# Products of 256 tokens with both parts of x side by side: ffn1's up product and three of four groups of the deep down products

## What is computed

```
def swiglu_ffn(h, w_in, w_out):                 # first block
    a, g = jnp.split(h @ w_in, 2, axis=-1)
    return (jax.nn.silu(a) * g) @ w_out

def gated_conv_ffn(x, w_gate, w_up, conv_w, conv_b, w_down):   # second block
    g = causal_dwconv3(x @ w_gate, conv_w) + conv_b
    return (jax.nn.silu(g) * (x @ w_up)) @ w_down
```

## Time and profile before

| | |
|---|---|
| time, median of 3 runs | 1600.87 us (1599.76 to 1603.91) |
| the profiled execution's own time | 1600.98 us |
| its span (first to last instruction) | 1599.8 us |
| mean granted TensorE clock | 0.994 of full speed |
| busy: PE, DVE, ACT | 98%, 56%, 43% |
| matmuls | 11195, about as many weight loads |
| chain that ended last | PE 88%, DVE 4%, ACT 2%, POOL 2% |

### The profile page before, as it was taken

One profiled execution on the slowest core, in us unless ns is written; L12 is line 12 of the kernel. 1 busy time (PEld: TensorE's weight loads), 2 busy tenths in 40 slices (PEclk: granted clock), 3 DMA queues, 4 the chain that ended last, 5 costly groups with the idle time before them and its releaser, 6 DMA issues.

```text
span 1599.8 us, 25708 instructions
## 1 busy us (share of the span) xinstructions
PE 1560.6 (98%) x11195; PEld 1386.1 (87%) x11195; DVE 901.0 (56%) x1176; ACT 682.0 (43%) x923; POOL 88.0 (6%) x124
## 2 busy tenths in 40 slices
PE   6999999999999999999999999999999999999998
PEld 4778866867888888878768999999999999999998
DVE  5422477463333433357866655568777656677763
ACT  4312476342212322235764444544545446555552
POOL 2210052000000000000000000034000000000000
PEclk8999999999999999999999999999999999999999
DMA  9864532745533232364134555565555554555551
GB/s 334 249 192 158 142 31 20 263 136 187 179 105 105 80 105 74 98 230 152 54 112 153 177 192 172 176 213 173 171 186 182 189 180 155 166 180 185 178 173 71
DMA packets 242976, 251.19 MB, mean 157 GB/s; under 512 B 4797, under 2 KB 240672, under 8 KB 242864
## 3 DMA queue, kind: packets, MB, share of 16 engines
q1 hardware_dynamic: 240080, 244.33, 46.2%
q0 software_dynamic: 2464, 5.09, 2.6%
q10 hardware_dynamic: 320, 0.13, 0.0%
HBM read 248.49 MB, written 1.05 MB: 156 GB/s over the span
## 4 chain that ended last, share of the span: by engine, by line
PE 88%; DVE 4%; ACT 2%; POOL 2%; issue 1%; DMA 1%; SPq 1%; DVEq 0%; ACTq 0%; POOLq 0%
PE psum L354 86%; PE psum L846 2%; DMA pre<-in_ada_w 1%; DVE sums L909 1%; POOL ptmp L1736 1%; DVE pt L923 1%; ACT wh L333 1%; DVE wl L340 1%; SPq L289 0%; DMA raw<-in_ada_w 0%; POOL ptmp L1735 0%; ACT scr L876 0%; DVE acc L1515 0%; POOL scr L1743 0%; ACT xh L624 0%
## 5 line engine op out<-in xcount | busy, mean ns | idle before, releaser
L354 PE MATMUL psum<-xh,wh 128*128 128x256 f32 (+1 forms) x1936 | 615.8, 318 | 5.0 <-DVE xl L668 2.8
L354 PE MATMUL psum<-xl,wh 128*128 128x256 f32 (+1 forms) x1936 | 609.3, 315 | 0.0
L354 PE MATMUL psum<-xh,wl 128*128 128x256 f32 (+1 forms) x1936 | 609.1, 315 | 0.0
L340 DVE TENSOR_TENSOR wl<-raw,wh 128x2048 fp32r<-128x2048 f32 (+1 forms) x186 | 419.1, 2254 | 273.1 <-ACT wh L333 272.9
L333 ACT ACTIVATE wh<-raw 128x2048 fp32r<-128x2048 f32 (+1 forms) x186 | 348.2, 1874 | 389.8 <-PE psum L354 385.0
L354 PEld LDWEIGHTS psum<-xh,wh 128*128 128x128 f32 x1936 | 370.2, 191 | 37.8 <-issue 10.0
L354 PEld LDWEIGHTS psum<-xh,wl 128*128 128x128 f32 x1936 | 370.2, 191 | 22.6
L354 PEld LDWEIGHTS psum<-xl,wh 128*128 128x128 f32 x1936 | 370.4, 191 | 21.9 <-issue 0.7
L354 PE MATMUL psum<-ah,wh 128*128 128x256 f32 (+1 forms) x704 | 217.9, 310 | 0.0
L354 PE MATMUL psum<-ah,wl 128*128 128x256 f32 (+1 forms) x704 | 217.9, 310 | 0.0
L354 PE MATMUL psum<-al,wh 128*128 128x256 f32 (+1 forms) x704 | 217.9, 310 | 0.0
(11 more groups left out here) (254 smaller groups left out, 1568.2 us busy)
## 6 DMA issues: line engine op xcount, KB each, us to landing
raw<-in_ffn_w_in SPq DMA_DIRECT2D x44, 1024.0 KB, 4.9
raw<-in_ada_w SPq DMA_DIRECT2D x25, 1024.0 KB, 5.3
pre<-in_ada_w SPq DMA_DIRECT2D x23, 1024.0 KB, 9.9
raw<-in_w_ffn_gate SPq DMA_DIRECT2D x22, 1024.0 KB, 5.2
raw<-in_w_ffn_up SPq DMA_DIRECT2D x22, 1024.0 KB, 5.2
raw<-in_ffn_w_out SPq DMA_DIRECT2D x16, 1024.0 KB, 5.0
raw<-in_w_ffn_down SPq DMA_DIRECT2D x16, 1024.0 KB, 5.0
raw<-in_na_w_qkv SPq DMA_DIRECT2D x12, 1024.0 KB, 5.6
```

The source lines that it names most:

```text
L340: dve.e.tensor_tensor(wl[:, c % NSPL, 0:z], raw[:, p % NRAW, 0:z], wh[:, c % NSPL, 0:z].bitcast(F32), ALU.subtract).then_inc(W.lo, 1)
L354: return pe.e.matmul(o, l, r, start=start, stop=stop, skip_group_check=shared)
```

## The change

Low and high part of x are placed side by side in one tensor (`x5`, `a1`; the addresses are those that they had). A new `group_wide` moves both at once: a matmul of the weights' high block by 512 columns (high part of x, then low part) into a whole bank, and one of the weights' low block by 256 columns into the first half of the same bank. So two matmuls and two weight loads stand where three and three stood; the number of columns is the same. The two halves of a bank have to be added afterwards, and the two halves m of a group now take a bank each.

It is used for the 22 groups of ffn1's up product and for the first three groups of D1, D2 and D3. The fourth group stays as it was, in bank 6 or as `DBANKS` says. ffn1's groups turn through three pairs of banks in place of six banks, and PE waits for the sum of group g-3. ACT and DVE now have work in every slot: in an even one ACT copies the second half bank into `scr`, DVE adds the first half to it, ACT takes tanh of the sum, DVE (tanh + 1) * a; in an odd one ACT copies the second half of g, DVE adds, DVE multiplies, ACT makes the high part, DVE the low part. In the down products DVE adds each half of the bank to the residual in turn. Some waits of later stages on banks are moved to match.

```diff
+        def group_wide(o, cs, x, ready, k_outer=False):
+            total, k0 = sum(weights[c][1] for c in cs), 0
+            for c in cs:
+                h, l = taken(c)
+                nk = weights[c][1]
+                for k, m in [(k, m) for k in range(nk) for m in range(2)] if k_outer else [(k, m) for m in range(2) for k in range(nk)]:
+                    ready(k0 + k)
+                    w = slice(m * P, (m + 1) * P)
+                    mm(o[m].rearrange("p (s n) -> p s n", s=2), h[:, k, w], x[:, :, k0 + k, :], k0 + k == 0, False, True)
+                    last = mm(o[m][:, 0:T], l[:, k, w], x[:, 0, k0 + k, :], False, k0 + k == total - 1, True)
+                last.then_inc(W.used, 1)
+                k0 += nk
...
 def down_pe(d, ready, ks=None):
             for i in range(4):
                 d.free(i)
-                group_T(halves(d.banks[i]), d.chunks(i), d.src[0], d.src[1], T, ready, k_outer=i == 0, ks=ks)
+                if d.wide is not None and i < 3:
+                    group_wide([psum[:, d.banks[i] + m, :] for m in range(2)], d.chunks(i), d.wide, ready, k_outer=i == 0)
+                    continue
+                group_T(halves(bank[d.banks[i]]), d.chunks(i), d.src[0], d.src[1], T, ready, k_outer=i == 0, ks=ks)
...
 def down_dve(d):
-                b = d.banks[i]
-                if d.gates is None:
+                b = bank[d.banks[i]]
+                if d.wide is not None and i < 3:
+                    parts = [psum[:, d.banks[i]:d.banks[i] + 2, s * T:s * T + T] for s in range(2)]
+                    for s in range(2):
+                        if s:
+                            dve.wait_ge(DN.half, d.at.half + d.per * (i + 1))
+                        done = DN.res if s else DN.half
+                        if d.gates is None:
+                            dve.e.tensor_tensor(pair(hT, i), parts[s], pair(hT, i), ALU.add).then_inc(done, 1)
+                        else:
+                            for m in range(2):
+                                k = 2 * i + m
+                                dve.e.scalar_tensor_tensor(hT[:, k, 0:T], parts[s][:, m, :], mod_col(*d.gates, k, 0), hT[:, k, 0:T], ALU.mult,
+                                                           ALU.add).then_inc(done, 1)
+                elif d.gates is None:
...
 def ffn1_pe():
             for g in range(22):
-                if g >= 6:
-                    pe.wait_ge(G1.g1 if g % 2 == 0 else G1.g2, (g - 6) // 2 + 1)
-                group_T(halves(ring[g]), [where["up1", g]], xh5, xl5, T, lambda k: pe.wait_ge(N.xl, 48 + k + 1), k_outer=g == 0)
+                if g >= 3:
+                    pe.wait_ge(G0.sum1 if (g - 3) % 2 == 0 else G0.sum2, (g - 3) // 2 + 1)
+                group_wide([bank[pairs1[g]], bank[pairs1[g] + 1]], [where["up1", g]], x5, lambda k: pe.wait_ge(N.xl, 48 + k + 1), k_outer=g == 0)
...
 def ffn1_act():
                 split_for(split_hi, c)
-                if g % 2:
-                    s = scr[:, p % 6, :]
-                    act.wait_ge(W.used, c + 1)
-                    if p >= 6:
-                        act.wait_ge(G1.lo, p - 5)
-                    act.e.activation(s, ring[g - 1][:, :], ACT.Tanh, scale=0.5).then_inc(G1.tanh, 1)
-                    act.wait_ge(G1.g2, p + 1)
-                    act.e.activation(ah1[:, 2 * p:2 * p + 2, :].rearrange("p k n -> p (k n)"), s, ACT.Copy).then_inc(G1.hi, 1)
+                act.wait_ge(W.used, c + 1)
+                if g % 2 == 0:
+                    t, u = tiles1(p)
+                    if p >= 3:
+                        act.wait_ge(G0.lo, 22 + p - 2)
+                    act.e.activation(two(t), parts1(g)[1], ACT.Copy).then_inc(G0.copy1, 1)
+                    act.wait_ge(G0.sum1, p + 1)
+                    act.e.activation(u, t, ACT.Tanh, scale=0.5).then_inc(G0.tanh, 1)
+                else:
+                    t, u = tiles1(p)
+                    act.wait_ge(G0.g1, 22 + p + 1)
+                    act.e.activation(two(u), parts1(g)[1], ACT.Copy).then_inc(G0.copy2, 1)
+                    act.wait_ge(G0.g2, 22 + p + 1)
+                    act.e.activation(ah1[:, 2 * p:2 * p + 2, :].rearrange("p k n -> p (k n)"), t, ACT.Copy).then_inc(G0.hi, 1)
             down_act(D1)
...
 def ffn1_dve():
-                if g % 2:
-                    s = scr[:, p % 6, :]
-                    dve.wait_ge(G1.tanh, p + 1)
-                    dve.e.scalar_tensor_tensor(s, s, 1.0, ring[g - 1][:, :], ALU.add, ALU.mult).then_inc(G1.g1, 1)
-                    dve.wait_ge(G1.g1, p + 1)
-                    dve.e.scalar_tensor_tensor(s, s, 0.5, ring[g][:, :], ALU.mult, ALU.mult).then_inc(G1.g2, 1)
-                    dve.wait_ge(G1.hi, p + 1)
-                    hi, lo = (t[:, 2 * p:2 * p + 2, :].rearrange("p k n -> p (k n)") for t in (ah1, al1))
-                    dve.e.tensor_tensor(lo, s, hi.bitcast(F32), ALU.subtract).then_inc(G1.lo, 1)
+                t, u = tiles1(p)
+                if g % 2 == 0:
+                    dve.wait_ge(G0.copy1, p + 1)
+                    dve.e.tensor_tensor(two(t), parts1(g)[0], two(t), ALU.add).then_inc(G0.sum1, 1)
+                    dve.wait_ge(G0.tanh, 22 + p + 1)
+                    dve.wait_ge(G0.sum1, p + 1)
+                    dve.e.scalar_tensor_tensor(t, u, 1.0, t, ALU.add, ALU.mult).then_inc(G0.g1, 1)
+                else:
+                    dve.wait_ge(G0.copy2, p + 1)
+                    dve.e.tensor_tensor(two(u), parts1(g)[0], two(u), ALU.add).then_inc(G0.sum2, 1)
+                    dve.wait_ge(G0.sum2, p + 1)
+                    dve.e.scalar_tensor_tensor(t, t, 0.5, u, ALU.mult, ALU.mult).then_inc(G0.g2, 1)
+                    dve.wait_ge(G0.hi, 22 + p + 1)
+                    hi, lo = (x[:, 2 * p:2 * p + 2, :].rearrange("p k n -> p (k n)") for x in (ah1, al1))
+                    dve.e.tensor_tensor(lo, t, hi.bitcast(F32), ALU.subtract).then_inc(G0.lo, 1)
```

More of the change, by code:

```diff
@@ L166, in program @@
         mixh1, mixl1 = at(0, "mixh1", [P, KT, T], F32R), at(8, "mixl1", [P, KT, T], F32R)
-        ah3, al3 = at(0, "ah3", [P, FT, T], F32R), at(22, "al3", [P, FT, T], F32R)
+        x5, a1 = at(78, "x5", [P, 2, KT, T], F32R), at(0, "a1", [P, 2, FT, T], F32R)
+        xh5, xl5 = (x5[:, s, :, :] for s in range(2))
+        ah1, al1 = ah2, al2 = ah3, al3 = [a1[:, s, :, :] for s in range(2)]
         yt, y = at(46, "yt", [P, KT, T]), at(54, "y", [P, 2, D])
@@ L1097, in o0_dve @@
             diag_dve(1, 4)
-        G0 = semaphores(nc, "ffn0", "tanh g1 g2 hi lo")
+        G0 = semaphores(nc, "ffn0", "tanh g1 g2 hi lo copy1 sum1 copy2 sum2")
         pairs0 = [(bank[0], bank[1]), (bank[2], bank[3]), (bank[6], bank[7])]
@@ L1463, in attention1_dve, with __init__ @@
             attention_dve(C1, last_values)
-        DN = semaphores(nc, "down", "res hi lo square sum sum2")
-        downs = [DN._make([0] * 6)]
+        DN = semaphores(nc, "down", "half res hi lo square sum sum2")
+        downs = [DN._make([0] * 7)]
         class Down:
-            def __init__(self, name, pieces, banks, src, free, gates, gain, to, n, double=False):
-                self.name, self.pieces, self.banks, self.src, self.free, self.gates = name, pieces, banks, src, free, gates
+            def __init__(self, name, pieces, banks, src, free, gates, gain, to, n, double=False, wide=None):
+                self.name, self.pieces, self.banks, self.src, self.free, self.gates, self.wide = name, pieces, banks, src, free, gates, wide
                 self.gain, self.to, self.n, self.double = gain, to, n, double
@@ L1477, in __init__ @@
                 self.at = downs[-1]
-                mine = (4 * self.per, 8 if to else 0, 8 if to and to[1] is not None else 0, 12 if double else 4, 4, 4 if double else 0)
+                mine = (3 * self.per if wide is not None else 0, 4 * self.per, 8 if to else 0, 8 if to and to[1] is not None else 0, 12 if double else 4, 4, 4 if double else 0)
                 downs.append(DN._make(a + b for a, b in zip(self.at, mine)))
@@ L1559, in down_dve @@
             next_sum(d, 3)
-        O1 = Down("o1", 1, bank[0:4], (xh4, xl4), lambda i: pe.wait_ge(A1.exp, base1.exp + 32), (1, 2), None, None, 3)
-        G1 = semaphores(nc, "ffn1", "tanh g1 g2 hi lo")
-        ring = [bank[i % 6] for i in range(26)]
+        O1 = Down("o1", 1, range(4), (xh4, xl4), lambda i: pe.wait_ge(A1.exp, base1.exp + 32), (1, 2), None, None, 3)
+        ring = [bank[i % 6] for i in range(22)]
+        DBANKS = (4, 0, 2, 6)
+        pairs1 = [(0, 2, 4)[g % 3] for g in range(22)]
         def free1(i):
-            p = 8 + i // 2
-            pe.wait_ge(G1.g1 if i % 2 == 0 else G1.g2, p + 1)
-        D1 = Down("dn1", 3, ring[22:26], (ah1, al1), free1, (1, 5), lambda k: small[:, 44 + k:45 + k], (xh5, xl5), 4, double=True)
+            if i < 3:
+                pe.wait_ge(G0.sum1 if i == 1 else G0.sum2, (10, 11, 11)[i])
```

(2 more changed lines are left out.)

31 lines of the change are left out of this document (15 added, 16 removed).

## The result

The changed kernel takes 1596.89 us in the median of 6 runs (1595.78 to 1598.73); the kernel before, run beside it, takes 1603.61 (1599.76 to 1604.53). The ratio is 0.9966, with a 95% interval of 0.9953 to 0.9978: faster by 5.5 us, where 8.3 were forecast. That ratio goes with the means of the six and six, 1597.19 and 1602.71; the two medians lie 6.7 us apart. The profiled execution took 1598.73 (span 1597.5, mean granted clock 0.993).

A forecast was written before the change was run, and what follows sets the result against it. PE was taken to bound ffn1 and D1, by columns plus 13.3 ns per matmul. Savings of 3.1 us (up) and 5.3 (downs), 8.4 taken as 8.3, led from 1600.98 to 1592.7, predicted median 1592.6; range 1590.0 to 1597.5.

The forecast's parts named there:

- the first term of the sum: PE, ffn1's up product and D1 to D3: each of 748 blocks saves 13.3 ns, 10.0 us in all.
- Starts 0.227 and 0.120 apart in turn: Sign expected in the profile after: spacing in us of PE's 512- and 256-column matmul starts in changed groups.
- the sign named for a wrong prediction: PE's 512-column matmuls standing more than 0.227 us apart, or gaps coming before chunk 10, would refute the forecast.
- The base: Whole kernel: savings were taken from the profiled 1600.98 us; the median shown was 1600.87.
- a longer ring: Rival, ffn1's up product: ACT and DVE's ring exceeds its rows; 0.1 us more per step gives 1601; chance 0.10.
- The moving side in two runs: Changed PE matmuls: 512 columns lying in two separate runs of 256 were taken to cost nothing extra.
- The rival of the jump: Changed PE matmuls: two runs cost 34 ns a jump, 15 us more, 1616 in all; chance 0.08.
- The ring: ffn1's up product: nine ACT and DVE steps take 11.50 us per pair, 0.41 longer than PE's 11.09.
- The gaps on PE: ffn1's up product: from about chunk 14 or 16 PE waits some 0.4 us per pair, 1.5 in all.
- The down products' side work: DVE's added 0.88 us per group in D1, 0.69 in D2 and D3, is hidden by idle time.
- The clock: Rival: small PE gaps in ffn1 halve the clock; five spells lose 7.5 us, giving 1600; chance 0.03.
- The fixed part: PE: 13.3 ns per matmul beyond its columns, saved with each matmul removed; the skill's 2.5 ns was rejected.

The follow-up runs named there:

- e5_ring: Changed kernel, but in ffn1's up product ACT and DVE do both splits of a pair in the even slot, none in the odd; 1593.96 us.
- e10_ring_kick: e5_ring plus a pair of small float32 matmuls ahead of the second wide group of D2 and D3; 1595.42 us, ratio 0.9953 to the kernel before.
- e12_ring_again: The same kernel as e5_ring, timed once more; 1595.44 us, ratio 0.9953 to the kernel before.
- e1_contig: Changed kernel, but 512-column matmuls move two neighbouring blocks of x's high part, one contiguous run (other products); 1594.97 us.
- e11_ring_longer: Changed kernel plus one unused 512-column DVE addition ahead of the sum in every even slot of ffn1's up product; 1603.42 us.

## Why the prediction came out as it did

**The step that failed** is the first term of the sum, "A block took 3 x 120.0 = 360.0 ns; now 226.7 + 120.0 = 346.7, 13.3 ns less." It adds two durations, each from a stage in which all matmuls have one length. In turn, the two lengths take 353.3 ns for much of the time, 6.7 less than before and not 13.3. On average the matmul of 512 columns is followed by the next start after 237 ns in the long rhythm (D1) and 232 in the short one, the one of 256 after 117 and 115: most of the difference lies with the long matmul, and neither rhythm is 226.7 and 120.0. The three downs were in the long rhythm throughout: 132 x 6.7 ns = 0.88 us each, measured 0.81, 0.88 and 0.88, forecast 1.76 (5.3 in all, measured 2.6). Where the short rhythm held, the term was right (D1 of e5_ring, e10_ring_kick and e12_ring_again). "Starts 0.227 and 0.120 apart in turn" held for the sum of the two alone, and only from 900.6 to 978.2; the sign named for a wrong prediction, 512-column matmuls more than 0.227 apart, is there. Why there are two rhythms stays open. What should have been a bound was not named: rows of one length don't show the cost of mixing lengths, and the bounds I took concerned the moving side's place alone.

**The base.** The forecast of 1592.6 was made against 1600.98 us. Beside the changed kernel the one before took 1603.61, and by the difference the forecast would read 1595.3. Of the 4.3 us between 1592.6 and 1596.9, 2.7 are that base: three executions, two of which happened to be among the quickest of the six. By the stages the rhythm in the downs is worth another 2.6. The two make 1.0 more than the miss, as the medians lie 6.7 us apart and the means, like the stages, only 5.5; with executions of one kernel 3 to 5 us apart, that much is chance. The time lies in the range all the same, but the upper part of the range was put there for a longer ring, and what used it was the rhythm.

**The moving side in two runs** costs nothing, as taken: e1_contig keeps D2 and D3 at 62.36 us without it. The rival of the jump is out, with its 34 ns.

**The ring** was right step by step: 11.52 for 11.50, DVE's split to its sum 920.83 - 918.62 = 2.21 for 2.20, the sum's successor to the high part 0.72, high part to split 0.54. It sets D1's start: 124.56 us after the stage's first matmul, forecast 124.5. The gaps on PE were fewer than forecast and began at chunk 18 of the stage, not at 14 or 16. This one, before chunk 20 of the stage, is the longest (TensorE timeline after):

```profile
978.20 0.28 PE L354 MATMUL psum<-x,wl 128*128 128x256 f32 x1
978.66 0.47 PE L354 MATMUL psum<-x,wh 128*128 128x512 f32 x1 [0.18 <-DVE wl L340]
978.96 0.28 PE L354 MATMUL psum<-x,wl 128*128 128x256 f32 x1
979.08 0.39 PE L354 MATMUL psum<-x,wh 128*128 128x512 f32 x1
```

978.66 - 978.20 is 0.46 where 0.12 is the rule: 0.34 lost. With 0.16 at 966.9 and 0.10 at 989.9 that makes 0.6 us, and the first block behind each takes 0.42 (979.08 - 978.66) for 0.35: 0.8 in all, not 1.5, because PE spent the rest in the long rhythm, 0.5 in groups 1 to 5 and 0.2 in the last two, hidden by the ring. The end of the stage, which the ring sets, came out right for that reason, although PE's own time was wrong.

**The down products' side work** is hidden, as costed. VectorE in D1 after (before: the earlier trace rows):

```profile
1005.95 1.79 DVE L1580 SCALAR_TENSOR_TENSOR hT<-psum,mod,hT 128x256 f32<-128x256 f32 x4
...
1013.60 2.29 DVE L340 TENSOR_TENSOR wl<-raw,wh 128x2048 fp32r<-128x2048 f32 x1 [3.41 <-ACT wh L333]
...
1021.57 1.79 DVE L1580 SCALAR_TENSOR_TENSOR hT<-psum,mod,hT 128x256 f32<-128x256 f32 x4
```

The sum takes 1.79 for 0.88, and DVE is still idle for 3.41 us before the split. The distance of two groups is 15.62, not 15.25: the rhythm again. From ACT's split at D1's end in the chain (1048.62, before 1049.16) to PE's next long piece (1099.44) are 50.82 us, before 50.80.

**The clock** stayed at 1.00 throughout ffn1's up product and D1, in after and with e11_ring_longer's gaps before each chunk (2.5 us of idle PE in the 90 from 900 to 990). The Trainium skill ("TensorE: Matmul & The Clock Gate", section A second HAM failure mode: psum-queue depth-cycling) warns of short idles; gaps of this length and distance did not bring it about here. The prediction read the earlier trace rows too far, though, when it said that the clock is 0.50 only where PE had idled for microseconds in a row: before the fall at 1062.4 PE stood idle for 0.9 us of the nine from 1053 to 1062, and before the one of after at 740.9 it was busy for all of the eleven from 730 to 741. Its price, 1.5 us for a spell of 3, fits the 1.6 and 1.5 measured.

**The fixed part.** In the short rhythm each matmul less gives the full 13.3 ns, in the long one half of it. The Trainium skill ("TensorE: Matmul & The Clock Gate", section Back-to-back issue gap) gives N / 2.4 GHz + 2.5 ns, by which the change had been worth 1.9 us; the trace fits it in neither rhythm. The prediction left out that the section calls this the gap of an isolated matmul and has another figure for a stream of weight loads and matmuls, about 131 ns at 512 columns; the 226.7 ns of ffn0 contradict that one too.

## What to carry to other kernels

A duration per instruction, read where all instructions are alike, is a bound and not a price once two kinds take turns: cost the mixture from a mixture, or keep half of the gain in the range. When two engines with hand-written orders hand work to each other in both directions, add up one turn of the ring, start to start, against the bound engine's period; busy shares of DVE and ACT in the stage of 69% and 50% (53.2 and 38.3 us of the 77 from 901 to 978) hid a ring that was longer than PE's period by 0.4 us in 11.1, and moving one split behind a wait took it away. Compare stages by their own first and last instructions: untouched stages moved the ends of two executions here by 3.3 us, over half of what the change was worth, and the granted clock of those stages told why.

## What the runs showed of the hardware that I had not expected

Matmuls of 512 and 256 columns in turn take 346.7 or 353.3 ns a pair, at full clock, in a state that lasts over hundreds of instructions, through the border of two stages, and that differed between two executions of the same program (14.15 and 13.87 us for 40 pairs at the same place). A wait of some tenths of a microsecond or one `fp32r` product of 8 columns can switch it, in either direction; small float32 matmuls between wide groups were followed by 346.7 each time (19 of 19), and a stage of 256 columns alone by 353.3 each time (25 of 25). With eight of one length and then eight of the other the pair takes 348.7 ns. What the state is stays open.

The granted clock fell to half for a few microseconds at places that differ between executions of the same or nearly the same program (187.9 and 740.9 us in after, not in before), once with PE busy without a break for the eleven microseconds ahead of it. Each such spell cost some 1.5 us.
